# A lead of its own for each weight piece, and the right halves of four plain units' rests added by a transfer

## The reference

```python
def swiglu(x, w_gu, w_down):
    g, u = jnp.split(x @ w_gu, 2, axis=-1)
    return (jax.nn.silu(g) * u) @ w_down
...
        h = h + swiglu(rms_norm(h, ffn_norm[layer]), ffn_w_gu[layer], ffn_w_down[layer])   # layer 0 and 1
```

## Time and profile before

| | |
|---|---|
| runs | 2214.72, 2214.83, 2216.0 us |
| the profiled execution | 2213.68 us, its span 2211.8 us |
| busy in the span | TensorE 2147.3 us, VectorE 1460.8, ScalarE 1082.7, GpSimd 320.9 |
| mean granted TensorE clock | 0.997 |
| pieces of the first fast feed-forward part | 511.40 to 772.54 us of the span |
| pieces of the second | 1133.64 to 1393.98 us |
| VectorE busy, 600 to 700 us | 90.28 us of 100 |

### The profile page before, as it was taken

How to read it: one execution, slowest core, us unless ns; L and a number is a source line. 1 busy time by engine, 2 the same in 40 slices (tenths; PEclk the granted TensorE clock), 3 DMA queues, 4 the chain that set the end, 5 groups by cost and what they waited for, 6 DMA issues and landing times.

```text
span 2211.8 us, 33448 instructions
## 1 busy us (share of the span) xinstructions
PE 2147.3 (97%) x12698; PEld 1836.8 (83%) x12698; DVE 1460.8 (66%) x2344; ACT 1082.7 (49%) x1700; POOL 320.9 (15%) x267
## 2 busy tenths in 40 slices
PE   9999999998999999999999999999999999999998
PEld 6788887788999978877889989878778778888887
DVE  6766666479999843455689999556666665555522
ACT  5445555345454544565444555355565554444312
POOL 0221222310000030002200000300111144222211
PEclk9999999999999999999999999999999999999999
DMA  3311111221222322201213222331221222222221
GB/s 140 115 58 39 58 39 39 74 91 65 96 96 96 125 92 89 79 36 39 96 65 107 96 96 100 130 132 58 72 72 39 72 97 96 98 101 102 96 95 57
DMA packets 31675, 185.00 MB, mean 84 GB/s; under 512 B 3104, under 2 KB 7712, under 8 KB 11312
## 3 DMA queue, kind: packets, MB, share of 16 engines
q1 hardware_dynamic: 29520, 175.48, 22.9%
q0 software_dynamic: 2016, 7.60, 1.0%
HBM read 178.84 MB, written 7.37 MB: 84 GB/s over the span
## 4 chain that ended last, share of the span: by engine, by line
PE 74%; DVE 13%; ACT 5%; issue 4%; DMA 2%; SPq 0%; DVEq 0%; POOL 0%; ACTq 0%; POOLq 0%
PE ps L2331 20%; PE ps L2333 19%; PE ps L2332 19%; DVE wl L1483 3%; DMA raw<-in_stream 2%; PE ps L2657 2%; PE ps L3148 1%; ACT wh L525 1%; PE ps L3091 1%; PE ps L3131 1%; PE ps L2651 1%; DVE wsum L1454 1%; ACT wh L657 1%; PE ps L3158 1%; PE ps L2923 1%
## 5 line engine op out<-in xcount | busy, mean ns | idle before, releaser
L2331 PE MATMUL ps<-xh,wh 128*128 128x512 f32 (+1 forms) x1616 | 610.3, 378 | 13.3 <-DVE act_up L1380 9.4
L2333 PE MATMUL ps<-xh,wl 128*128 128x512 f32 (+1 forms) x1616 | 584.0, 361 | 0.0
L2332 PE MATMUL ps<-xl,wh 128*128 128x512 f32 (+1 forms) x1616 | 582.8, 361 | 0.0
L2331 PEld LDWEIGHTS ps<-xh,wh 128*128 128x128 f32 x1616 | 306.0, 189 | 63.4 <-issue 12.1
L2333 PEld LDWEIGHTS ps<-xh,wl 128*128 128x128 f32 x1616 | 305.1, 189 | 48.0
L2332 PEld LDWEIGHTS ps<-xl,wh 128*128 128x128 f32 x1616 | 306.0, 189 | 42.4 <-issue 4.3
L1229 DVE TENSOR_TENSOR wl<-raw,wh 128x2048 fp32r<-128x2048 f32 x92 | 212.8, 2313 | 175.7 <-ACT wh L525 175.6
L525 ACT ACTIVATE wh<-raw 128x2048 fp32r<-128x2048 f32 x92 | 175.9, 1912 | 161.1 <-PE ps L2333 160.8
L2331 PE MATMUL ps<-part_h,wh 128*128 128x256 f32 (+1 forms) x672 | 221.7, 330 | 6.0 <-DVE hT L1520 3.9
L2333 PE MATMUL ps<-part_h,wl 128*128 128x256 f32 (+1 forms) x672 | 220.3, 328 | 0.0
L2332 PE MATMUL ps<-part_l,wh 128*128 128x256 f32 (+1 forms) x672 | 219.8, 327 | 0.0
(11 more groups left out here) (427 smaller groups left out, 4069.0 us busy)
## 6 DMA issues: line engine op xcount, KB each, us to landing
raw<-in_stream SPq DMA_DIRECT2D x158, 1024.0 KB, 4.8
hankd<-tabd SPq DMA_DIRECT2D x1, 3072.0 KB, 17.3
hank<-hankd POOLq DMA_DIRECT2D x4, 768.0 KB, 5.1
hT<-in_xT SPq DMA_DIRECT2D x4, 512.0 KB, 6.1
keepd<-hT POOLq DMA_DIRECT2D x1, 2048.0 KB, 10.1
hT<-keepd POOLq DMA_DIRECT2D x8, 256.0 KB, 4.8
out<-hT SPq DMA_DIRECT2D x8, 256.0 KB, 2.5
raw<-in_stream SPq DMA_DIRECT2D x2, 512.0 KB, 7.7
```

The costliest lines, as they stand in the source:

```text
L2331: pe.matmul(out, w_hi, a_hi, start=start, stop=False, skip_group_check=goes_on)
L2332: pe.matmul(out, w_hi, a_lo, start=False, stop=False, skip_group_check=goes_on)
L2333: return pe.matmul(out, w_lo, a_hi, start=False, stop=stop, skip_group_check=goes_on)
```

## The change

There are three parts.

**Leads.** HI_LEAD and LO_LEAD are now tables by k. Pieces k = 5 and 6, which are the last two quarters of `raw`, are rounded earlier, piece 0 later. The sums are made one by one, seven or six pieces ahead. New lists count the roundings and rests in their new order (`HIGHS`, `RESTS`).

**Smaller bursts.** `pair_lo` is cut into `pair_lo` (two rests) and `pair_sums_lo` (two rests, a turn later), `gated` runs three turns after the last piece instead of two, and the pair sums and hidden chunks that depend on it are a turn later too. `pair_hi` signals after its second copy instead of its third.

**Half of a rest by a transfer.** For plain units 2 to 5 ScalarE writes the negated rounded right half into `wl` first, then `wh`. VectorE makes only the left half of the rest. GpSimd issues a transfer from memory that adds the raw weights onto the negated rounded part. TensorE waits for it before the 9th block of the unit.

```diff
-HI_LEAD = 5
-SUM_LEAD = 6
+HI_LEAD = {0: 4, 2: 5, 1: 5, 4: 5, 3: 5, 5: 6, 6: 7}
+LO_LEAD = {0: 3, 2: 4, 1: 4, 4: 4, 3: 4, 5: 5, 6: 5}
...
-PAIR_SUMS_AT.update({DONE_AT[GATE_AT[2 * m + 1]] + 3: m for m in (3, 5, 6, 7)})
+PAIR_SUMS_AT.update({DONE_AT[GATE_AT[2 * m + 1]] + 4: m for m in (3, 5, 6, 7)})
...
+def due(p, lead):
+    return [(j, k) for i, (j, k) in enumerate(ORDER) if i - lead[k] == p]
...
+                def split_hi_half(n):
+                    u = u0 + n
+                    act.wait_ge(raw_landed[u % 2], 16 * (u // 2) + 16)
+                    act.wait_ge(units_used, u - 1)
+                    right = slice(UNIT // 2, UNIT)
+                    act.activation(wl[:, u % 2, right], raw[:, u % 2, right], ACT.Copy, scale=-1.0)
+                    act.activation(wh[:, u % 2, :], raw[:, u % 2, :], ACT.Copy).then_inc(hi_made, 1)
...
                 def gate_up(n):
                     if n < PLAIN - 2:
-                        split_hi(u0 + n + 2)
+                        split_hi_half(n + 2)
...
-                    act.activation(part_h[:, 3 * i, :], act_of(2 * m + 1), ACT.Copy)
-                    act.activation(part_h[:, 3 * i + 1, :], ssq[:, :], ACT.Copy).then_inc(hid_hi_made, 1)
+                    act.activation(part_h[:, 3 * i, :], act_of(2 * m + 1), ACT.Copy).then_inc(hid_hi_made, 1)
+                    act.activation(part_h[:, 3 * i + 1, :], ssq[:, :], ACT.Copy)
...
-                        if p + HI_LEAD < len(ORDER):
-                            hi(*ORDER[p + HI_LEAD])
+                        for q in due(p, HI_LEAD):
+                            if q not in ORDER[:LEAD + 1]:
+                                hi(*q)
...
+                def split_lo_half(n):
+                    u, left = u0 + n, slice(0, UNIT // 2)
+                    dve.wait_ge(hi_made, u + 1)
+                    dve.tensor_tensor(wl[:, u % 2, left], raw[:, u % 2, left], wh[:, u % 2, left].bitcast(F32), ALU.subtract).then_inc(lo_made, 1)
...
                 def pair_lo(m):
                     i = m % 4
+                    dve.wait_ge(hid_hi_made, FC * f + 2 * m + 1)
...
+                def pair_sums_lo(m):
...
+                def sums(p):
+                    for ahead, kind, make in ((7, 2, first_sum), (6, 2, second_sum), (6, 3, difference), (7, 5, last_sum)):
+                        j, k = ORDER[p + ahead] if p + ahead < len(ORDER) else (None, None)
+                        if k == kind and j:
+                            make(j)
...
-                        j, k = ORDER[p - 2] if 1 < p <= len(ORDER) + 1 else (None, None)
+                        j, k = ORDER[p - 3] if 2 < p <= len(ORDER) + 2 else (None, None)
                         if j in GATES and k == 6:
                             gated(j)
...
                 gate_up(5)
+                last_sum(0)
                 products()
...
+            def half_rests(f):
+
+                for n in range(2, PLAIN):
+                    u, right = U0[FAST[f]] + n, slice(UNIT // 2, UNIT)
+                    landed, count = half_rest_by_dma(f, n)
+                    pool.wait_ge(hi_made, u + 1)
+                    if count > 16:
+                        pool.wait_ge(landed, count - 16)
+                    pool.dma_start(wl[:, u % 2, right], io["stream"][u][:, right], accum_op=ALU.add).then_inc(landed, 16)
+
             sum_squares("ffn0")
+            half_rests(0)
...
+                        if j >= 2 and i == KC:
+                            pe.wait_ge(*half_rest_by_dma(f, j))
```

More of the change, by code:

```diff
@@ L163 @@
 PAIR_SUMS_AT = {1: 1, 5: 2, DONE_AT[DOWN_AT[3]] + 1: 4}
-PAIR_SUMS_AT.update({DONE_AT[GATE_AT[2 * m + 1]] + 3: m for m in (3, 5, 6, 7)})
+PAIR_SUMS_AT.update({DONE_AT[GATE_AT[2 * m + 1]] + 4: m for m in (3, 5, 6, 7)})
 HIDDEN_AT = {DONE_AT[DOWN_AT[7]] + 1: REST, DONE_AT[DOWN_AT[7]] + 2: REST + 1}
-HIDDEN_AT.update({DONE_AT[GATE_AT[n]] + 3: n for n in range(REST + 2, FC)})
+HIDDEN_AT.update({DONE_AT[GATE_AT[n]] + 4: n for n in range(REST + 2, FC)})
+def due(p, lead):
+    return [(j, k) for i, (j, k) in enumerate(ORDER) if i - lead[k] == p]
+ROUNDED = ORDER[:LEAD + 1] + [q for p in range(len(ORDER)) for q in due(p, HI_LEAD) if q not in ORDER[:LEAD + 1]]
+RESTED = ORDER[:LEAD] + [q for p in range(len(ORDER)) for q in due(p, LO_LEAD) if q not in ORDER[:LEAD]]
+HIGHS = {q: sum(k != 6 for _, k in ROUNDED[:i + 1]) for i, q in enumerate(ROUNDED)}
+RESTS = {q: sum(k != 6 for _, k in RESTED[:i + 1]) for i, q in enumerate(RESTED)}
 def gu_count(f, n):
@@ L417, in build @@
         last_piece = ORDER[-1]
-        each = {part_hi: SPLITS[last_piece] + 3, part_lo: SPLITS[last_piece] + 3, prod_done: SPLITS[last_piece],
+        parts = DONE[last_piece]
+        each = {part_hi: parts + 3, part_lo: parts + 3, prod_done: parts,
                 weights_summed: 4 * len(STREAM), forked: FORKS[last_piece], joined: JOINS[last_piece], normed: 8,
@@ L1523, in products @@
                     for p in range(len(ORDER) + 5):
-                        if p + LEAD < len(ORDER):
-                            lo(*ORDER[p + LEAD])
-                        elif p < len(ORDER):
+                        for q in due(p, LO_LEAD):
+                            if q not in ORDER[:LEAD]:
+                                lo(*q)
+                        if len(ORDER) <= p + LEAD < len(ORDER) + 4:
                             down_lo(p + LEAD - len(ORDER))
-                        if p + SUM_LEAD < len(ORDER):
-                            sums(*ORDER[p + SUM_LEAD])
+                        sums(p)
                         j, k = ORDER[p - 1] if 0 < p <= len(ORDER) else (None, None)
@@ L1559, in ffn_fast @@
                 pair_lo(0)
+                pair_sums_lo(0)
                 gate_up(4)
[L1561 to L1564, removed]
+                first_sum(0)
+                second_sum(0)
+                for q in ORDER[:LEAD]:
+                    lo(*q)
+                difference(0)
                 gate_up(5)
+                last_sum(0)
                 products()
@@ L2225, in _ @@
             sum_squares("ffn1")
+            half_rests(1)
             sum_squares("lat")
```

59 lines of the change are left out of this document (31 added, 28 removed).

## The result

The changed kernel takes 2191.6 us (median of 4 runs, 2191.11 to 2191.86), the kernel before 2215.4 beside it: ratio 0.9891, 95% interval 0.9874 to 0.9909. That is 24 us, 1.1%. The profiled span is 2189.2 us for 2211.8.

What follows compares the result with a forecast made beforehand. TensorE's waits on a late VectorE, itself delayed by landing loads, were taken as the bound in the pieces. Gains 8.9 + 8.2 + 3.0 + 3.0 = 23.1 us turned 2213.68 into 2190.6 profiled, forecast 2192 us median, range 2184 to 2206.

Steps and rivals of the forecast that it cites:

- Pieces 33 to 123: Later streamed pieces of both feed-forward parts: nearly all TensorE waits go, winning 8.9 and 8.2 us.
- The residual of 2.0 us: Loss expected to remain in pieces 33 to 123 of each part: 0.4, three of 0.4 to 0.5, and 0.3 elsewhere.
- the walk: VectorE's new order added up by measured operation times, giving the TensorE waits left before `up_right(8)` and later `gated`.
- Pieces 0 to 32: First streamed pieces of each part: TensorE reaches piece 33 at 566.5, not 569.54, winning 3.0 us per part.
- The transfer: Half rest by adding transfer in plain units: costed at nothing, landing taken as 5.1 us.
- a cover of 13 us: Time from issuing unit 5's adding transfer to TensorE's 9th block, which hides its landing: 13.1 us.
- Signs: Expected in the later profile: `raw` waits under 8 us, gaps about 4.0 before (0,2), clock near 0.62, no block 9 wait.
- the three waits of TensorE: TensorE's waits for `up_right`, `gated` and `add_half` over the whole kernel: together under 10 us of 24.0.
- Rival 1: VectorE stays late in the pieces by its own rate, only half its waits going: 2203 us, chance 0.18.
- Rival 2: In the pieces, later `gated` lengthens ten TensorE waits by 0.94 us each, 9.4 lost: 2210 us, chance 0.08.
- Rival 3: Late transfer before block 9 of plain units 2 to 5, 8 us per us over 13.1: 2225 us, chance 0.09.
- 0.86: Whole kernel: chance given to it being faster, beside 0.05 for the same and 0.09 for slower.

Runs made afterwards that it cites:

- transfer_only: The kernel before plus only the adding transfer, with old leads and order in the pieces; ratio 0.9996 to the kernel before.
- no_transfer: The changed kernel without the adding transfer; its median equals the changed kernel's to 0.1 us.
- short_loads: The kernel before with each looped weight load cut from 1024 to 256 KB, order unchanged; 13.4 us faster than the kernel before.
- gated_early: The changed kernel with `gated` one turn sooner and ScalarE's copy of (0,0) ahead of chunk 5's scaling and SiLU; median 2185.5 us.

## Why the prediction was right

I forecast 2192 us, and it was 2191.6. The total is closer than its terms: the pieces gave 22.3 us for the 23.1 forecast, and the profiled execution took 2191.11 us for 2190.6. By the steps of the sum:

- **Pieces 33 to 123**, 8.9 + 8.2 us: measured 8.8 + 8.1. The residual of 2.0 us is 2.1: 0.34 before (8,6), which waits for `up_right(8)`, and 0.50 before each of (12,0), (14,0) and (16,0), which wait for `gated` (0.35 us idle in the trace, and the restart); the walk had 0.4 and 0.4 to 0.5. This walk let VectorE run without a wait for ScalarE's roundings, and in these pieces it has one, of 0.6 us.
- **Pieces 0 to 32**, 3.0 + 3.0 us: measured 3.2 + 2.2. The copy starts at 516.56 (516.5), piece 33 at 566.77 (566.5), the wait at (2,0) is 1.74 (1.7). The gap is 3.6 us and not 4.0 only because the pieces begin 0.45 us later. Mis-sized was the second part: the same gap of 3.6 us was followed by 5.27 us for the 24 matmuls where I had taken 4.4 for both; all of them ran at 1.2 GHz.
- **The transfer**, nothing: `transfer_only` is 0.9996, `no_transfer` equals the changed kernel to 0.1 us in the median. Landing 6.1 us, inside 4 to 9, and over the row of 5.1 for 768 KB that I took the earlier trace rows. With a cover of 13 us the difference does not matter. The fit of the Trainium skill (DMA: Bandwidth & Descriptors, section Anatomy of one DMA) gave an estimate of 3.2 us for that size; the trace has 6.1 for an adding one, and does not agree.
- **Signs**: ScalarE's waits for `raw` 0 (under 8); the three waits of TensorE 6.7 us (under 10); the gaps 3.6 us (about 4.0); no wait at block 9 of a plain unit. Missed was the clock behind the second gap: 0.50, where I had said near 0.62 (0.64 in the first part).

The size was right, the story of its cause only half. I wrote that VectorE's lateness comes from the landing. A landing 1.9 us sooner gives 4.4 us of the 10.9 (`short_loads`), the leads alone 9.1, and the smaller bursts, which I had given no gain of their own in these pieces but a cost at `gated`, win 5.4 us with the landing left late. The gains of leads and bursts do not add: 9.1 and 5.4 alone, 8.8 together. What the runs show is a stage in which VectorE is busy 127.8 us of 131.6 (the count by the steps was 127.5). That it therefore can't make up what it loses to one late thing before the next comes (the landing, the sums, four pair rests in a row) fits these numbers, but it is a reading, and no run shows it by itself.

Rival 1 (VectorE's rate) was wrong as a price. As a mechanism it is right for the first 33 pieces, where VectorE is busy 50.80 of 51.55 us once the copy is out of the way. Rival 2's cost exists, though smaller than its price: `gated` standing behind two operations that could wait costs the changed kernel 3.6 us of span, 5.1 in the medians. Rival 3's price was 1.5 times what I gave it, through the clock. In the chances, "most of 2" does not fit the sum: 0.86 leaves 0.03 of rival 2's 0.08.

Left open: why the slower clock lasted 5.27 us behind a gap of 3.6 us in one part and less in the other; which of the lead's two moves, the rest of (j,6) or `last_sum`, is worth more, since no run split them; and which edit among the smaller bursts wins the 5.4 us, though in the changed kernel the later `gated` costs time.

## What to carry to other kernels

In a stage where one engine is nearly full (VectorE 92% of the 91 pieces before, 97% after), don't expect the gains of two edits to add: here they did not. Take one group away alone, and then the other, before crediting either. Walk the order of the late engine by measured steps from a waited-for operation to the next; that walk gave the residual of the 91 pieces to 0.1 us. It forecasts the new order, though, and does not prove why the old one was late. And put what TensorE waits for ahead of what it doesn't: `gated` one turn sooner was the cheapest gain. The best kernels run are the two with it, 2185.5 and 2186.5 us.

## What was not expected of the hardware

The length of one gap does not tell what TensorE's clock does behind it. In the bursts-only kernel an idle time of 2.50 us left the clock alone, and one of 2.56 us some 20 us later was followed by about 3 us at 1.2 GHz:

```profile
515.64 0.36 PE L2382 MATMUL ps<-t_h,wh 128*128 128x256 f32 x1 [2.50 <-DVE wl L1520]
...
515.64:518.56 2.92, 2.92 (x25) 1.00 0.02 6
...
535.35 0.55 PE L2382 MATMUL ps<-xh,wh 128*128 128x256 f32 x1 [2.56 <-DVE act_up L1410]
...
536.00:537.00 1.00, 1.00 (x7) 0.50 0.73 303
```

In `gated_early` an idle time of 1.96 us had the same sequel. Where the shorter gap keeps the clock and the longer one does not, a us of gap is worth more than a us: before (0,2) the bursts-only kernel loses 2.7 us with its gap, the changed kernel 5.4 (first part) with one 1.1 us longer.

An adding transfer of 512 KB, issued by GpSimd, landed in 5.6 to 7.2 us, longer than a plain load of 1024 KB that SyncE issued (4.8 on the page). How much of that is the addition is not shown: plain transfers issued by GpSimd took 4.9 us for 256 KB and 5.3 for 768 on the same page.
